# A hybrid decoder layer on one core: memory projections in seven products, a row buffer in the score column, norm rows by matmuls, larger table pieces and an earlier low-rank pair

## What is computed

```python
proj = h @ w_in                       # HGRN2 q,f,i,g | attention q | ckv | index q,k,w | two gates
ya = hgrn2_branch(...) @ w_branch_a
yb = dsa_branch(...) @ w_branch_b     # 64 chosen keys, low-rank keys and values from rms_norm(ckv), T5 bias
mix = (sigmoid(gate_a) * ya + sigmoid(gate_b) * yb) @ w_mix_out
h = layer_norm(ALPHA * h + mix, ln1_g, ln1_b)
k, v = mem @ w_ck, mem @ w_cv         # 256 memory positions, 4 heads of 512
ca = softmax(q k / sqrt(512)) v @ w_co,   q = h @ w_cq
h = layer_norm(ALPHA * h + ca, ln2_g, ln2_b)
# PEER: 8 heads pick 16 of 128*128 experts each, per token
y = sum_e gate_e * gelu(h . peer_u[e]) * peer_v[e]      # 128 experts per token
out = layer_norm(ALPHA * h + y, ln3_g, ln3_b)
```

## Time and profile before

| | us |
|---|---|
| median of 3 runs | 3068.3 (3062.9 to 3069.97) |
| the profiled execution | 3066.08 |
| its span in the trace | 3064.3 |

### The profile page before, as it was taken

How to read it: one execution, slowest core, us unless ns; L and a number is a source line. 1 busy time by engine, 2 the same in 40 slices (tenths; PEclk the granted TensorE clock), 3 DMA queues, 4 the chain that set the end, 5 groups by cost and what they waited for, 6 DMA issues and landing times. The chain is left out here.

```text
span 3064.3 us, 37080 instructions
## 1 busy us (share of the span) xinstructions
PE 2556.3 (83%) x16040; PEld 2153.9 (70%) x16040; DVE 1358.3 (44%) x1735; ACT 412.9 (13%) x882; POOL 824.3 (27%) x536
## 2 busy tenths in 40 slices
PE   8999999999999999888987989589666766676555
PEld 7899899999889899888987978488552222222221
DVE  0122001001100074785545455554698857556666
ACT  1122000021000011111100220010100012111111
POOL 0000000000000021233322234222256665665652
PEclk9999999999999999999998999799888877887777
DMA  8876378876847789999999999999999999999997
GB/s 330 275 293 243 138 288 292 305 284 252 329 143 273 260 345 424 425 416 409 403 423 403 396 421 387 422 421 424 399 389 422 422 422 422 422 422 421 422 422 308
DMA packets 126929, 1096.37 MB, mean 358 GB/s; under 512 B 13440, under 2 KB 22064, under 8 KB 28080
## 3 DMA queue, kind: packets, MB, share of 16 engines
q1 hardware_dynamic: 50512, 542.08, 44.9%
q0 software_dynamic: 76256, 551.94, 43.9%
HBM read 1084.52 MB, written 9.44 MB: 357 GB/s over the span
## 5 line engine op out<-in xcount | busy, mean ns | idle before, releaser
L602 PE MATMUL PS<-arena 128*128 128x128 f32 (+1 forms) x13696 | 1851.9, 297 | 93.7 <-DMA arena<-units 77.6
L602 PEld LDWEIGHTS PS<-arena 128*128 128x128 f32 x13696 | 1762.5, 193 | 177.5 <-DMA arena<-units 76.5
L975 PE MATMUL PS<-arena 128*128 128x512 f32 x880 | 500.3, 728 | 292.3 <-DMA arena<-peer_v,arena 277.1
L1400 DVE CUSTOM_DVE_ANT_0 arena<-arena 128x2048 f32<-128x2048 f32 x256 | 586.8, 2292 | 311.9 <-DMA arena<-peer_u,arena 304.2
L975 PEld LDWEIGHTS PS<-arena 128*128 128x128 f32 x880 | 199.5, 236 | 592.5 <-issue 543.1
L567 POOL DMA_INDIRECT arena<-peer_u,arena x256 | 407.6, 1592 | 718.9 <-DVE arena L1400 481.2
L567 POOL DMA_INDIRECT arena<-peer_v,arena x256 | 405.6, 1585 | 542.9 <-DVE arena L1410 321.3
L1410 DVE SCALAR_TENSOR_TENSOR arena<-arena 128x2048 f32<-128x2048 f32 x146 | 343.3, 2351 | 151.0 <-DMA arena<-peer_v,arena 147.4
L992 ACT ACTIVATE arena<-PS 128x512 f32<-128x512 f32 (+2 forms) x154 | 84.5, 549 | 1354.6 <-PE PS L602 1221.0
L1365 ACT ACTIVATE arena<-arena 128x128 f32<-128x128 f32 x110 | 44.2, 402 | 592.2 <-PE PS L975 591.9
L633 PE MATMUL PS<-arena 128*128 128x128 f32 x166 | 32.5, 338 | 90.7 <-DVE arena L1581 34.4
(11 more groups left out here) (190 smaller groups left out, 1080.2 us busy)
## 6 DMA issues: line engine op xcount, KB each, us to landing
arena<-units SPq DMA_DIRECT2D x243, 2048.0 KB
arena<-w_ukv SPq DMA_DIRECT2D x16, 512.0 KB, 12.1
arena<-ln_rows SPq DMA_DIRECT2D x6, 1024.0 KB, 13.9
arena<-ln_rows POOLq DMA_DIRECT2D x4, 1024.0 KB, 19.2
arena<-peer_u,arena POOLq DMA_INDIRECT x256, 23.8
arena<-peer_v,arena POOLq DMA_INDIRECT x256, 24.0
rb_scratch<-arena POOLq DMA_DIRECT2D x1, 3072.0 KB, 37.3
arena<-rb_scratch SPq DMA_DIRECT2D x12, 256.0 KB, 11.8
```

The costliest lines, as they stand in the source:

```text
L602: ins = mm(bank[:, first:first + rhs.shape[1]], lhs, rhs, start=k == 0, stop=k == KT - 1)
L975: ins = mm(Y[c], diag[:, n % 4 * P:(n % 4 + 1) * P], rows[b][:, c * 512:(c + 1) * 512], start=n == first_used[tb], stop=False, skip_group_ ...
L1400: mark(v.tensor_tensor_reduce(rows[b], rows[b], h_tok[tb], 1.0, 0.0, ALU.mult, ALU.add, dots[tb][:, e:e + 1]), dot_done, s + 1)
```

## The change

Six edits:

1. **Keys and values by seven products.** A CK or CV unit is taken as a 2 x 2 block product (depth halves by column halves by position halves) and done with 7 products of 8 matmuls of 128 columns (`seven`, `product`) in place of 32 matmuls of 256 columns. VectorE forms four sums of the memory once (`sum_memory`), four sums of each unit's weights (`sum_weights`, 128 x 1024 each), and three combinations of the results (`combine`, 128 x 128 each); ScalarE copies three partial results and the last block (`seven_out`).
2. **A seventh row buffer** in `scores` (2048 columns, unused between the choices of block 0 and block 1), open to arrivals from number 46 to 18 before `LATE`. `SOON` goes from 74 to 78, `LATE` from 202 to 206, and VectorE has one more `turn(4)`, after the sparse attention's last group of block 1.
3. **Norm rows by matmuls.** The six rows of 1 MB become 24 loads of 2 KB onto single partitions (`load_vectors`); TensorE spreads a row with four matmuls of depth 1 against a row of 1/128 (`spread_row`), ScalarE copies it out times 128 (`row_out`). Block 0's four GpSimd loads stay.
4. **Table pieces of 6 KB:** ScalarE writes the table row four times side by side, and the same 3 MB go out from the same 16 partitions in runs of 6 KB.
5. **Early low-rank pair:** units `U_CKV` and `U_IK` of block 1 are loaded and computed after CO of block 0, before `turn_scaled` and PQ.
6. The first bias loads wait for `acc_done` (the index scores are summed) and no longer for `sel_done`; the three small norm rows of block 1 are loaded at `U_CQ + 2`.

```diff
-SOON = 74
+SOON = 78
+SCORES = SLOTS + 2 * RING
+OPEN, SHUT = 46, 18
+def load_order():
+    order = [(0, u) for u in units_of(0) if u < U_PQ] + [(1, U_CKV), (1, U_IK)]
+    order += [(0, u) for u in units_of(0) if u >= U_PQ]
+    return order + [(1, u) for u in units_of(1) if u not in (U_CKV, U_IK)]
...
-        b = min(range(SLOTS if n < LATE else count), key=lambda i: taken[i])
+        free = list(range(SLOTS if n < LATE else SCORES))
+        if OPEN <= n < LATE - SHUT:
+            free.append(SCORES)
+        b = min(free, key=lambda i: taken[i])
...
-                    sp.wait_ge(sel_done, tb + 1)
+                    sp.wait_ge(acc_done, groups_before(tb + 1) if tb == 0 else 12)
...
-            pool.dma_start(rb_scratch, table[0:16, 512:896].unsqueeze(1).to_broadcast([16, P, 384])).then_inc(rb_out, 16)
+            pool.dma_start(rb_scratch.rearrange("h (r n) x -> h r (n x)", n=4),
+                           table[0:16, 512:2048].unsqueeze(1).to_broadcast([16, P // 4, 1536])).then_inc(rb_out, 16)
...
+            def seven(name, j):
...
+                pe.wait_ge(w_landed[p % RING], 16 * (p // RING + 1))
+                pe.wait_ge(evac_done, s - 3 if j == 0 else s - 1)
+                product(name, halves(w, 0, 0), halves(mem_t, 0, 0), bank_q, True).then_inc(product_done, 1)
+                if j == 0:
+                    pe.wait_ge(evac_done, s - 2)
+                    pe.wait_ge(mem_summed, 4)
+                else:
+                    pe.wait_ge(combined, 3 * n - 2)
+                pe.wait_ge(w_summed, 4 * n + 1)
+                product(name, s1, t1, bank_r, True).then_inc(product_done, 1)
...
+                pe.wait_ge(combined, 3 * n + 2)
+                product(name, halves(w, 1, 1), t4, bank_q, False).then_inc(proj_done, 1)
...
+            def spread_row(row, banks):
+                norm, n = divmod(row, 2)
+                if n == 0:
+                    pe.wait_ge(vec_in, 128 * (norm + 1))
+                pe.wait_ge(lnrow_sb, 4 * row)
+                for c in range(4):
+                    at = slice(VECTOR_AT[n][c // 2], VECTOR_AT[n][c // 2] + 1)
+                    ins = mm(banks[c], mean_m[at, :], row_vectors[norm][c % 2][at, :], start=True, stop=True)
+                ins.then_inc(lnrow_ps, 1)
...
+                if tb == 0:
+                    low_rank(1)
                 for q in range(4):
                     turn_scaled(tb, q)
...
+            def sum_weights(name, j):
...
+                for i, (dst, a, b, how, used) in enumerate(((s1, w01, w11, ALU.add, 2), (s2, s1, w00, ALU.subtract, 3),
+                                                            (s4, w10, s2, ALU.subtract, 4), (w01, w00, w01, ALU.subtract, 0))):
+                    if j and used:
+                        dve.wait_ge(product_done, 6 * (n - 1) + used)
+                    mark(v.tensor_tensor(dst, a, b, how), w_summed, 4 * n + i + 1)
...
+                if tb == 0:
+                    sum_memory()
+                    sum_weights("CK", 0)
+                    for j in range(UPM):
+                        if j + 1 < UPM:
+                            sum_weights("CK", j + 1)
+                        combine("CK", j)
+                        if j < 4:
+                            last_steps[j](q)
```

More of the change, by code:

```diff
@@ L176 @@
 ROWS = row_buffers()
+LAST_SCORES = [row for row in ARRIVALS if ROWS[row][0] == SCORES][-1]
 def group(tb):
@@ L282, in trunk_layer @@
         vc_t = inside(rows_area, 8192, 4096)
-        table = inside(rows_area, 8192, 1024)
-        rows = [inside(rows_area, n * D, D) for n in range(SLOTS)] + [inside(w_ring, n * D, D) for n in range(2 * RING)]
+        table = inside(rows_area, 8192, 2048)
+        rows = [inside(rows_area, n * D, D) for n in range(SLOTS)] + [inside(w_ring, n * D, D) for n in range(2 * RING)] + [scores]
         fin_g, fin_b, fin_x = R_M, R_X, R_O
         sums = [acc, inside(S, 4096, D)]
+        row_vectors = [[inside(S, 6656 + 512 * n, 512) for n in range(2)]] * 2 + [[inside(R_B, 512 * n, 512) for n in range(2)]]
         a_ex, a_pr = R_M, R_B
@@ L421, in load_low_rank, with load_vectors @@
                 sp.dma_start(wukv[pair % 2], w_ukv[pair]).then_inc(ukv_in[pair % 2], 16)
+            def load_vectors(norm):
+                for n in range(2):
+                    for c in range(4):
+                        place = VECTOR_AT[n][c // 2]
+                        sp.dma_start(row_vectors[norm][c % 2][place:place + 1, :],
+                                     ln_rows[2 * norm + n:2 * norm + n + 1, c * 512:(c + 1) * 512]).then_inc(vec_in, 16)
             def load_kept(m):
@@ L857, in trunk @@
                     for j in range(UPM):
-                        unit(0, U_CK + j, (0, "CK", j), 0, False, mem_t, width=SEQ)
+                        seven("CK", j)
                         if j < 4:
@@ L1068, in hg_body @@
                         act.wait_ge(rb_ps, 1)
-                        mark(fn(table[0:16, 512:896], B[3][0:16, 0:384], ACT.Copy), rb_sb, 1)
+                        for n in range(4):
+                            ins = fn(table[0:16, 512 + 384 * n:896 + 384 * n], B[3][0:16, 0:384], ACT.Copy)
+                        mark(ins, rb_sb, 1)
                     turned_keys(tb)
@@ L1181, in rows_out, with row_out @@
                 evacuate(tb, name, j, yz[j % 2], bank_of(tb, name, j))
+            def row_out(row, banks):
+                act.wait_ge(lnrow_ps, row + 1)
+                for c in range(4):
+                    fn(spread_rows[row][:, c * 512:(c + 1) * 512], banks[c], ACT.Copy, scale=float(P)).then_inc(lnrow_sb, 1)
             def rstd(tb):
@@ L1308, in trunk @@
                     rows_out(tb, "MIX", 0, j)
+                    if tb and j in (1, 2):
+                        row_out(j - 1, B)
                 rstd(tb)
@@ L1334, in trunk @@
                     rows_out(tb, "CO", 1, j)
+                    if tb and j in (1, 2):
+                        row_out(j + 1, B)
                 load_root()
@@ L1754, in trunk @@
                 first_norm(tb)
+                if tb == 0:
+                    combine("CV", 0, (2,))
+                    for j in range(1, UPM):
+                        sum_weights("CV", j)
+                        combine("CV", j)
                 if tb:
```

273 lines of the change are left out of this document (195 added, 78 removed).

## The result

The change made the kernel slower by a little: 3070.8 us median (3067.8 to 3076.7) against 3066.4 (3061.3 to 3070.0) of before, a ratio of 1.0018 with a 95% interval of 1.0012 to 1.0023. The prediction said 3043.6, range 3022 to 3060. The profiled execution has a span of 3071.9 us where before had 3064.3.

The account below looks back on a forecast made before the run. It took TensorE to bound the kernel up to the first gather and DMA after it. First gather +5.2, bytes -19.9, bias -6 and buffer -4 summed to -24.7 us, giving 3043.6 us, range 3022 to 3060.

Parts of the forecast that it names:

- rival (b): DMA holes behind the first gather don't close, bias and buffer give nothing, norm-row copies cost: 3058 us; chance 0.15.
- Bytes, -19.9: Behind the first gather, 8.39 MB fewer (pair's units, four norm rows) at 422 GB/s: -19.9 us.
- Keys, +10.3: Key units before the first gather: shorter units -10.6, first-unit stall +18.4, half-clock restart +2.5: +10.3 us.
- Rival (d): Weight sums run at half rate on strided halves of a unit, slowing keys and values: 3089 us; chance 0.05.
- Values, -10.6: Value units before the first gather: 1.33 us less a unit, nothing new late: -10.6 us, at worst -6.
- Pair, +5.5: Low-rank pair computed after CO, ahead of the first gather: +5.5 us, bounds +3 and +8.
- Table pieces, 0: Table write in 6 KB runs: 16 source partitions limit it, not run length: 0 us, bound -9.3.
- Early bias, -6: Block 1's first bias loads issued before selection ends, most of two DMA holes close: -6 us, bounds 0 and -8.4.
- Seventh buffer, -4: One more row in flight where VectorE holds the buffers: -4 us, bounds 0 and -9.
- Four rows, 0: The extra four V rows taken in block 1 only change places: 0 us.
- (a): Rival: the table write does speed up with longer runs, -9.3 us, giving 3034.3 us; chance 0.15.
- (c): Rival: last norm's rows count in full (-5.0) and DMA holes close nearly all (-7): 3031 us; chance 0.09.

Follow-up runs that it names:

- a_nopair: The changed kernel with the low-rank pair of block 1 back at the head of block 1: 3059.8 us, ratio to before 0.9978.
- v_one: The changed kernel with the first key unit's sums and copies and first value unit's copies earlier, late pair, 1.5 KB table runs: 3040.0 us, 0.9917 to before.
- b_bytes: The kernel before with SyncE's six norm-row loads read onto one partition, not 128, so fewer bytes cross: 3062.9 us, ratio to before 0.9989.
- a_early: The changed kernel with memory sums and first key unit's weight sums moved on VectorE ahead of the fourth quad's gate: 3060.3 us, ratio to before 0.9980.
- a_table: The changed kernel with the table written in runs of 1.5 KB again: 3067.5 us, ratio to before 1.0000.
- a_bias: The changed kernel with a block's first bias loads waiting for the selection again: 3071.7 us, ratio to before 1.0014.
- a_six: The changed kernel without the seventh row buffer, the additional four rows in block 1 kept: 3075.7 us, ratio to before 1.0031.
- a_soon74: The changed kernel with SOON back at 74 and without block 1's additional four rows, seventh buffer kept: 3075.1 us, ratio to before 1.0028.

## Why the prediction was wrong

**What bounds the kernel.** The failed step. From 411 GB/s between 1103 and 2290 I took it that DMA sets the pace there, so that a byte removed is worth 1/422 GB/s. The runs showed instead that 4.19 MB of norm rows were worth 3.4 us (0.6 to 6.4) and the pair's 4.19 MB nothing in block 1, and not 9.9 each. A full DMA says here only that somebody always wants more: the ring of three units and the row buffers are refilled ahead as soon as they are free. TensorE with its units and VectorE with its rows wait for each other at every quad. In the kernel before, TensorE's longest wait for the products was 8.1 us:

```profile
1239.27 1.11 PE L633 MATMUL PS<-arena 128*128 128x128 f32 x4 [8.07 <-DVE arena L1581]
```

The removed pair put TensorE 11 us ahead, its units kept their two thirds of DMA, VectorE got its rows no faster (one in 7.4 us, 5.1 of them waiting), and the lead was stood off at 1256:

```profile
1256.47 1.12 PE L742 MATMUL PS<-arena 128*128 128x128 f32 x4 [24.59 <-DVE arena L1756]
```

Meanwhile ring and buffers were full and DMA fell to 308 GB/s, a hole that before didn't have there (425 GB/s from 1250 to 1290). Before, then after:

```profile
1250.00:1290.00 40.00, 40.00 (x294) 37.87 (x293) 31.80 (x76) 2.13 (x4) 11.81 (x7) 1.00 1.01 425
```

```profile
1250.00:1270.00 20.00, 13.53 (x102) 13.54 (x103) 15.67 (x36) 5.82 (x8) 5.83 (x3) 0.72 0.77 308
```

Every run with the early pair and 16 KB loads has such a wait there (23 to 25 us), and none with the late pair has (a_nopair 9.8, v_one 8.7). This was named in the prediction's last sentence as what would make it wrong, an unchanged rate with new holes, and rival (b) came near it with GpSimd's queue in VectorE's order; but both kept the 19.9 us for the bytes.

**Bytes, -19.9.** About -3 for the norm rows (b_bytes) and nothing that the spread of block 1 would show for the pair (a_nopair). The last norm's rows at zero were right.

**Keys, +10.3.** Right in mechanism and size. The stall was forecast at 305.1 - 285.4 = 19.7 us and was 19.70; a key unit was forecast at 12.65 and took 12.67. By the selection of block 0 the kernel was 13.4 us late, 3.8 of it from the table: +9.6. The restart behind the stall cost less than the 2.5 us put down for it, an estimate of 1.6: 96 instructions took 12.43 us, and 96/112 of 12.67 are 10.86. Rival (d), strided sums at half rate, didn't come: five sums took 6.26 us.

**Values, -10.6.** -7.0. The units are 1.3 us shorter as worked out, but the first stands 2.75 us for ScalarE's copy (L1256), which is behind the norm's root on that engine:

```profile
853.11 7.08 PE L696 MATMUL PS<-arena 128*128 128x128 f32 x61 [2.75 <-ACT arena L1256]
```

I had ordered VectorE's steps around MIX and not ScalarE's. The same omission was in the key unit, hidden under the 19.7 us, and showed in a_early.

**Pair, +5.5.** +7.8, within its bounds. The wait on the peer keys' load came close as foreseen, and was real: 2.48 us at 1104.4, with the keys landing some 23.5 us after CO and not 21.9. That is nearly the whole difference. a_nopair took 9.0 us off the first gather.

**Table pieces, 0.** +3.8 in the trace; 2 to 4 by a_table. The prediction bounded this from 0 to -9.3 and left the loss out. That the length of the runs doesn't limit the write was right: 106 GB/s between 108 and 118 us where the earlier trace rows has 102, in both cases almost nothing but the write. That the 16 partitions limit it no run here shows; none changed their number.

```profile
108.00:118.00 10.00, 10.00 (x89) 9.71 (x88) 0.51 (x1) 0.60 (x1) 0.00 (x0) 1.00 0.99 106
```

The write kept its pace, and its packets, 4.6 KB before (1.02 MB in 222) and 6.1 KB after (1.06 MB in 172), only kept the engines from the units for longer.

**Early bias, -6.** 0 (a_bias, 0.04% with some 0.11% to each side). I priced the time at which SP is let go and not when its unit lands.

**Seventh buffer, -4.** About -4 (a_six), inside block 1, with an uncertainty as large.

**Four rows, 0.** 0 to -3 (a_soon74): they do change places, about 8 us in against 9 us out.

**Norm rows by matmul, 0.** TensorE takes 1.99 us a row and not 4.1, ScalarE 2.07, and no wait of more than 1.4 us on either. Nothing speaks against the term; no run takes it alone.

**The sum.** First gather 14.2; bytes of the norm rows -3.4; pair behind the first gather +3.3 (12.3 by the ratios less 9.0, no more than the spread); bias 0 to +1; buffer -4.0; rows -3.1. That is +7 to +8 where +5.5 was measured (1.0018), with 3 to 4 us of uncertainty in every term behind the first gather, so that the agreement is partly luck. The first gather holds the loss: 9 us of it were not in the forecast (table 3.8, values 3.6, pair 2.3, keys -0.7), and behind it 29.9 us of expected gain were 7 to 9.

Of the chances: (a) was wrong in sign, (c) expected more where there was less, (b) was the nearest and too small, and the 0.05 for slower rested on (d), the wrong mechanism. The measured 3070.8 lies above them all but (d).

## What to carry to other kernels

A DMA share near 1 in a stretch with prefetch does not show that bytes set its pace. Look at whether the consumers at its end wait for DMA or for each other; cut the bytes alone, in one run, before counting them. Where two queues compete, look at the size of their packets: here it set their shares, and favouring the rows paid where VectorE was late (early pair) and cost time where TensorE was (late pair). A stall that is moved off one engine's order waits in the next engine's: follow every producer of the stalled instruction, copies too, before pricing its removal.

## What was not expected of the hardware

In block 1 two full queues alternated packet for packet (970 and 972), so that cutting one queue's runs from 16 KB to 8 KB moved its share from 66 to 52% at an unchanged total (424 and 421 GB/s). They did not alternate at the start of the table write: for some 14 us the units' queue moved next to nothing with a unit outstanding. The write, limited to 102 to 106 GB/s, cost the other queue more in 6 KB runs than in 1.5 KB runs: 3.03 MB (changed) and 3.80 MB (a_table) in the same 28 us.
